# Cross attention of a two-layer decoder trunk: plain fp32 matmuls replaced by three fp32r passes over high and low parts

## The reference

```python
def memory_attention(h, m, wq, wkv, wo):
    q = (h @ wq).reshape(B, S, X_HEADS, X_HEAD_DIM).astype(F32)
    kv = (m @ wkv).reshape(B, M, 2, X_HEADS, X_HEAD_DIM).astype(F32)
    s = jnp.einsum('bshe,bmhe->bhsm', q, kv[:, :, 0]) * (X_HEAD_DIM ** -0.5)
    p = jax.nn.softmax(s, axis=-1)
    o = jnp.einsum('bhsm,bmhe->bshe', p, kv[:, :, 1]).reshape(B, S, D_MODEL)
    return o.astype(h.dtype) @ wo
```

## Time and profile before

| | us |
|---|---|
| median of 3 runs (lowest to highest) | 1506.36 (1506.22 to 1506.47) |
| the profiled execution's own time | 1506.58 |
| its span in the profile | 1504.5 |
| TensorE (PE) busy | 1483.1 |
| VectorE (DVE) busy | 882.4 |
| ScalarE (ACT) busy | 634.4 |
| GpSimd (POOL) busy | 380.3 |

### The profile page before, as it was taken

How to read it: one execution, slowest core, us unless ns; L and a number is a source line. 1 busy time by engine, 2 the same in 40 slices (tenths; PEclk the granted TensorE clock), 3 DMA queues, 4 the chain that set the end, 5 groups by cost and what they waited for, 6 DMA issues and landing times.

```text
span 1504.5 us, 19092 instructions
## 1 busy us (share of the span) xinstructions
PE 1483.1 (99%) x7842; PEld 1267.1 (84%) x7842; DVE 882.4 (59%) x1010; ACT 634.4 (42%) x883; POOL 380.3 (25%) x272
## 2 busy tenths in 40 slices
PE   8999999999999999999999999999999999999997
PEld 7878898888898888888898888988888988888886
DVE  5345556724367666575982465756245585756658
ACT  6335424524344343443562454335344352434344
POOL 2001720300053422315030028102001715151422
PEclk9999999999999999999999999999999999999999
DMA  8333131431223424152343232135203342433402
GB/s 288 90 98 101 53 112 65 150 122 54 94 106 115 137 85 162 62 168 99 112 133 119 64 95 86 67 105 175 84 29 112 112 147 79 141 110 112 140 28 98
DMA packets 83237, 162.09 MB, mean 108 GB/s; under 512 B 3664, under 2 KB 19792, under 8 KB 83152
## 3 DMA queue, kind: packets, MB, share of 16 engines
q1 hardware_dynamic: 81712, 158.35, 31.5%
q10 hardware_dynamic: 1440, 2.53, 0.5%
HBM read 158.78 MB, written 2.10 MB: 107 GB/s over the span
## 4 chain that ended last, share of the span: by engine, by line
PE 94%; DVE 2%; DMA 1%; ACT 1%; issue 1%; POOL 0%; SPq 0%; POOLq 0%; DVEq 0%; ACTq 0%
PE proj L688 26%; PE proj L690 25%; PE proj L689 25%; PE work L888 2%; PE work L690 2%; PE work L688 2%; PE work L689 2%; PE work L717 2%; PE work L867 2%; PE work L753 1%; DMA w_raw<-in_x_wkv_dram 1%; PE work L764 1%; PE work L743 1%; PE work L842 1%; PE work L821 0%
## 5 line engine op out<-in xcount | busy, mean ns | idle before, releaser
L1379 DVE TENSOR_TENSOR w_lo<-w_raw,w_hi 128x2048 fp32r<-128x2048 f32 (+1 forms) x103 | 234.8, 2280 | 274.9 <-ACT w_hi L1078 274.6
L688 PE MATMUL proj<-hT_hi,w_hi 128*128 128x512 f32 (+1 forms) x800 | 298.5, 373 | 0.0
L689 PE MATMUL proj<-hT_lo,w_hi 128*128 128x512 f32 (+1 forms) x800 | 297.7, 372 | 0.0
L690 PE MATMUL proj<-hT_hi,w_lo 128*128 128x512 f32 (+1 forms) x800 | 297.7, 372 | 0.0
L1078 ACT ACTIVATE w_hi<-w_raw 128x2048 fp32r<-128x2048 f32 (+1 forms) x103 | 185.3, 1799 | 234.2 <-PE proj L690 232.2
L688 PE MATMUL proj<-w_hi,hT_hi 128*128 128x512 f32 (+1 forms) x640 | 238.5, 373 | 3.5 <-ACT kmT L1182 2.2
L690 PE MATMUL proj<-w_hi,hT_lo 128*128 128x512 f32 (+1 forms) x640 | 232.3, 363 | 0.0
L689 PE MATMUL proj<-w_lo,hT_hi 128*128 128x512 f32 (+1 forms) x640 | 231.8, 362 | 0.0
L690 PEld LDWEIGHTS proj<-hT_hi,w_lo 128*128 128x128 f32 x800 | 150.7, 188 | 26.3
L689 PEld LDWEIGHTS proj<-hT_lo,w_hi 128*128 128x128 f32 x800 | 150.7, 188 | 26.1
L688 PEld LDWEIGHTS proj<-hT_hi,w_hi 128*128 128x128 f32 x800 | 150.7, 188 | 26.0
(11 more groups left out here) (197 smaller groups left out, 2446.3 us busy)
## 6 DMA issues: line engine op xcount, KB each, us to landing
w_raw<-in_w_up_dram SPq DMA_DIRECT2D x32, 1024.0 KB, 5.7
w_more<-in_w_down_dram SPq DMA_DIRECT2D x24, 1024.0 KB, 5.1
w_raw<-in_w_in_dram SPq DMA_DIRECT2D x28, 768.0 KB, 4.4
w_raw<-in_x_wkv_dram SPq DMA_DIRECT2D x15, 1024.0 KB, 5.1
w_raw<-in_w_out_dram SPq DMA_DIRECT2D x8, 1024.0 KB, 5.0
w_raw<-in_x_wq_dram SPq DMA_DIRECT2D x8, 1024.0 KB, 5.1
w_raw<-in_x_wo_dram SPq DMA_DIRECT2D x8, 1024.0 KB, 5.1
w_hs<-in_w_down_dram SPq DMA_DIRECT2D x8, 1024.0 KB, 5.1
```

The source lines that it names most:

```text
L688: nc.tensor.matmul(dst, l_hi, r_hi, start=first, stop=False, skip_group_check=more)
L689: nc.tensor.matmul(dst, l_hi, r_lo, start=False, stop=False, skip_group_check=more)
L690: return nc.tensor.matmul(dst, l_lo, r_hi, start=False, stop=last, skip_group_check=more)
L1379: nc.vector.tensor_tensor(w_lo[:, slot, :, 0:cols], w_raw[:, raw, :, 0:cols], w_hi[:, slot, :, 0:cols].bitcast(F32), ALU.subtract).then_in ...
```

## The change

The scores and values of the cross attention are made in three fp32r passes. For this the queries, the keys, the values and the transposed probabilities each get a high and a low part. New on ScalarE: one copy of `kmT` (2048 elements in each partition). New on VectorE in each layer: one subtraction for `kmT_lo` (2048), 8 for `qx_lo`, 4 for `vm_lo` and 8 for `xpT_lo` (512 each). A bank of `proj` used by `vm` and `qx` jobs, and bank 2 of `work`, are now free when VectorE has made the low part, and no longer when ScalarE has copied.

The values are made in 8 rounds, round r = (two token tiles r // 2, head r % 2 of the pair): 2 chunks by 2 memory tiles by 3 passes of 256 columns. A round stands three steps behind the scores, not two, so there is a step 10; it stands after the first tile of the second block of `wo0`. On ScalarE the order in a step is now `hT_hi`, copy, exps. Lines left out are declarations of semaphores, start counts and the like; `...` in a `rearrange` stands for its pattern.

```diff
+X_SPLIT_JOBS = ("qx0", "qx1")
+VM_SPLIT_JOBS = ("vm0", "vm1")
 # bank_users(): the last user of a bank of proj
+            elif name in X_SPLIT_JOBS:
+                last[t] = ("qx_lo", 4 * X_SPLIT_JOBS.index(name) + t)
+            elif name in VM_SPLIT_JOBS:
+                last[t] = ("vm_lo", MT * VM_SPLIT_JOBS.index(name) + t)
+ROUND_LAG = 3
+def round_of(r):
+    both, i = divmod(r, 2)
+    pair, t = divmod(2 * both, T)
+    first = pair * BK + 2 * i
+    return both, i, slice(first, first + 2), slice(t * P, (t + 2) * P)
...
-        vm = part("vm", 8, [P, MT, D])
+        vm_hi = part("vm_hi", 8, [P, MT, D], F32R)
+        vm_lo = part("vm_lo", 0, [P, MT, D], F32R)
-        x_probsT = part("x_probsT", 20, [P, 2, 512])
+        xpT_hi = [part(f"xpT_hi{i}", at, [P, 2 * MT, 2 * P], F32R) for i, at in enumerate((20, 40))]
+        xpT_lo = nc.alloc_sbuf_tensor_at("xpT_lo", [P, 2, 2 * MT, 2 * P], F32R, offset=mem_start)
-        qxT = part("qxT", 24, [P, KC, S])
+        kmT_lo = part("kmT_lo", 60, [P, KC, MEM], F32R)
+        kmT_hi = nc.alloc_sbuf_tensor_at("kmT_hi", [P, KC, MEM], F32R, offset=hs_start)
+        qx_hi = part("qx_hi", 24, [P, KC, S], F32R)
+        qx_lo = part("qx_lo", 44, [P, KC, S], F32R)
...
 # TensorE, x_scores (the head of a unit, its two chunks k)
+                    pe.wait_ge(km_lo, nth(km_lo, l, 1))
-                pe.wait_ge(emptied, nth(emptied, l, TILES_BEFORE["qx1" if pair == 0 else "wo0"]))
+                pe.wait_ge(qx_lo_done, nth(qx_lo_done, l, 4 * (pair + 1)))
-                        mm = nc.tensor.matmul(work[:, u % 2, i * MEM:(i + 1) * MEM], qxT[:, c, t * P:(t + 1) * P],
-                                              kmT[:, c, :], start=(k == 0), stop=(k == 1))
+                        mm = three_passes(work[:, u % 2, i * MEM:(i + 1) * MEM], qx_hi[:, c, tokens], qx_lo[:, c, tokens],
+                                          kmT_hi[:, c, :], kmT_lo[:, c, :], k == 0, k == 1)
 # x_turn
-                pe.wait_ge(x_copied, nth(x_copied, l, u))
+                pe.wait_ge(xp_lo_done, nth(xp_lo_done, l, u))
 # x_weigh(l, r)
+                pe.wait_ge(xp_lo_done, nth(xp_lo_done, l, 2 * both + 2))
                 pe.wait_ge(x_lo, nth(x_lo, l, r))
+                pe.wait_ge(vm_lo_done, nth(vm_lo_done, l, 2 * MT))
+                for n, k in enumerate(range(chunks.start, chunks.stop)):
                     for j in range(MT):
+                        mm = three_passes(work[:, 3, n * 2 * P:(n + 1) * 2 * P], vm_hi[:, j, at], vm_lo[:, j, at],
+                                          xpT_hi[both % 2][:, i * MT + j], xpT_lo[:, both % 2, i * MT + j],
+                                          j == 0, j == MT - 1)
 # x_step
-                if 2 <= j < XUNITS + 2:
-                    x_weigh(l, j - 2)
+                if ROUND_LAG <= j < XUNITS + ROUND_LAG:
+                    x_weigh(l, j - ROUND_LAG)
 # before_tile of wo0 and its second block; after_tile
-                    pe.wait_ge(x_lo, nth(x_lo, l, (b - FIRST_BLOCK["wo0"]) * T + t + 1))
+                    pe.wait_ge(x_lo, nth(x_lo, l, (b - FIRST_BLOCK["wo0"]) * T + 2 * (t // 2) + 2))
+                if b == FIRST_BLOCK["wo0"] + 1 and t == 0:
+                    x_step(l, XUNITS + 2)
...
 # ScalarE, x_step: the old order was exps, hT_hi, copy
+                if j >= ROUND_LAG:
+                    act.wait_ge(x_weighed, nth(x_weighed, l, j - ROUND_LAG + 1))
+                    nc.scalar.activation(hT_hi[:, chunks, tokens], work[:, 3].rearrange(...), ACT.Copy).then_inc(x_hi, 1)
+                if 1 <= j <= XUNITS:
+                    act.wait_ge(x_turned, nth(x_turned, l, u + 1))
+                    act.wait_ge(x_weighed, nth(x_weighed, l, 2 * both - 2))
+                    nc.scalar.activation(xpT_hi[both % 2][:, :, u % 2 * P:(u % 2 + 1) * P],
+                                         work[:, 2].rearrange(...), ACT.Copy).then_inc(x_copied, 1)
                 if j < XUNITS:                                    # the two exps, as before
...
 # ScalarE, before_block
+                if b == FIRST_BLOCK["qx0"] + 1:
+                    act.wait_ge(turned, nth(turned, l, 2 * TURNED["n2", T - 1] + 2))
+                    nc.scalar.activation(kmT_hi[:], kmT[:], ACT.Copy).then_inc(km_hi, 1)
 # VectorE, x_step: first in the step
+                if 2 <= j <= XUNITS + 1:
+                    dve.wait_ge(x_copied, nth(x_copied, l, u + 1))
+                    nc.vector.tensor_tensor(xpT_lo[:, u // 2 % 2][dst], work[:, 2].rearrange(...),
+                                            xpT_hi[u // 2 % 2][dst].bitcast(F32), ALU.subtract).then_inc(xp_lo_done, 1)
 # VectorE, new helpers
+            def vm_low(l, name, t):
+                dve.wait_ge(emptied, nth(emptied, l, TILES_BEFORE[name] + t + 1))
+                nc.vector.tensor_tensor(vm_lo[:, t, at], proj[:, t], vm_hi[:, t, at].bitcast(F32),
+                                        ALU.subtract).then_inc(vm_lo_done, 1)
+            def qx_low(l, name, t):
+                dve.wait_ge(emptied, nth(emptied, l, TILES_BEFORE[name] + t + 1))
+                nc.vector.scalar_tensor_tensor(out=qx_lo[:, c], in0=proj[:, t], scalar=XD ** -0.5,
+                                               in1=qx_hi[:, c].bitcast(F32), op0=ALU.mult,
+                                               op1=ALU.subtract).then_inc(qx_lo_done, 1)
 # VectorE, after_tile: first of all
+                for name in X_SPLIT_JOBS:
+                    if b == FIRST_BLOCK[name] + KB - 1:
+                        qx_low(l, name, t)
+                for name in VM_SPLIT_JOBS:
+                    if b == FIRST_BLOCK[name] + KB - 1:
+                        vm_low(l, name, t)
 # VectorE, before_block
+                if b == FIRST_BLOCK["qx0"] + 1:
+                    dve.wait_ge(km_hi, nth(km_hi, l, 1))
+                    nc.vector.tensor_tensor(kmT_lo[:], kmT[:], kmT_hi[:].bitcast(F32), ALU.subtract).then_inc(km_lo, 1)
```

More of the change, by code:

```diff
@@ L486, in trunk @@
         qk_lo = counted("qk_lo", 2 * PAIRS)
+        qx_lo_done = counted("qx_lo_done", 2 * 4)
+        km_hi = counted("km_hi", 1)
+        km_lo = counted("km_lo", 1)
         den_turned = counted("den_turned", UNITS)
@@ L509, in trunk @@
         x_turned = counted("x_turned", XUNITS, 2)
-        x_copied = counted("x_copied", XUNITS, 1)
+        x_copied = counted("x_copied", XUNITS)
+        xp_lo_done = counted("xp_lo_done", XUNITS, 1)
+        vm_lo_done = counted("vm_lo_done", 2 * MT)
         x_weighed = counted("x_weighed", XUNITS, 2)
@@ L861, in x_scores @@
                     pe.wait_ge(turned_lo, nth(turned_lo, l, 2 * TURNED["n2", T - 1] + 2))
-                pe.wait_ge(emptied, nth(emptied, l, TILES_BEFORE["qx1" if pair == 0 else "wo0"]))
+                    pe.wait_ge(km_lo, nth(km_lo, l, 1))
+                pe.wait_ge(qx_lo_done, nth(qx_lo_done, l, 4 * (pair + 1)))
                 pe.wait_ge(x_exped, nth(x_exped, l, u - 1))
+                tokens = slice(t * P, (t + 1) * P)
                 for i in range(2):
@@ L876, in x_turn, with x_weigh @@
                 mm.then_inc(x_turned, 1)
[L878 to L886, removed]
+            def x_weigh(l, r):
+                both, i, chunks, _ = round_of(r)
+                pe.wait_ge(xp_lo_done, nth(xp_lo_done, l, 2 * both + 2))
+                pe.wait_ge(x_lo, nth(x_lo, l, r))
+                pe.wait_ge(vm_lo_done, nth(vm_lo_done, l, 2 * MT))
+                for n, k in enumerate(range(chunks.start, chunks.stop)):
                     for j in range(MT):
-                        mm = nc.tensor.matmul(work[:, 3, k * P:(k + 1) * P], vm[:, j, (pair * BK + k) * P:(pair * BK + k + 1) * P],
-                                              x_probsT[:, u % 2, (i * MT + j) * P:(i * MT + j + 1) * P],
-                                              start=(j == 0), stop=(j == MT - 1))
+                        at = slice(k * P, (k + 1) * P)
+                        mm = three_passes(work[:, 3, n * 2 * P:(n + 1) * 2 * P], vm_hi[:, j, at], vm_lo[:, j, at],
+                                          xpT_hi[both % 2][:, i * MT + j], xpT_lo[:, both % 2, i * MT + j],
+                                          j == 0, j == MT - 1)
                 mm.then_inc(x_weighed, 1)
@@ L1045, in _ @@
                                     pe.wait_ge(qk_lo, nth(qk_lo, l, user[1] + 1))
+                                elif user[0] == "vm_lo":
+                                    pe.wait_ge(vm_lo_done, nth(vm_lo_done, l, user[1] + 1))
+                                elif user[0] == "qx_lo":
+                                    pe.wait_ge(qx_lo_done, nth(qx_lo_done, l, user[1] + 1))
                                 else:
@@ L1061, in _ @@
         def _(act):
-            start_counts(act, emptied, p_copied, c_copied, x_exped, x_copied)
+            start_counts(act, emptied, p_copied, c_copied, x_exped)
             act.dma_start(gains[:, GAIN_SLOT["mem"]], norm_g[0:1, GAIN["mem"]].broadcast_to([P, D])).then_inc(gain_loaded["mem"], 16)
```

(30 more changed lines are left out.)

7 lines of the change are left out of this document (4 added, 3 removed).

## The result

The changed kernel takes 1508.89 us (median of 20 runs, 1508.34 to 1508.96), the kernel before beside it 1506.30 (1506.11 to 1506.49). The ratio is 1.0016, with an interval of 1.0010 to 1.0023: 2.6 us slower, where 2.8 were forecast. So the change did save matmul time, and new waits of TensorE gave back more than it saved.

The account below looks back on a forecast made before the run. TensorE, busy for 99% of the span, bounds the kernel. Per layer −5.04 us of matmuls, +4.1 of step waits and +2.4 of vm waits give +1.4; two layers +2.8 on 1506.36: 1509.2 us, range 1504.0 to 1512.0.

Parts of the forecast that it names:

- A pass of 256 columns takes 0.120: Cross-attention scores and values: 0.120 us per fp32r pass, saving 5.04 us per layer, 10.1 in two.
- rival 3: Cross-attention matmuls: passes start 0.109 us apart by the page's rule, giving 1506.6 us, no change; chance 0.05.
- The vm jobs wait 2.4 us a layer: Start of vm1 and qx0: TensorE waits for vm_low behind VectorE's list, 1.87 and 0.32 us plus restarts.
- Transposes 0, 1 and 5 wait 0.9, 1.2 and 1.7: Steps 1, 2 and 6 of cross attention: TensorE waits 0.90, 1.20 and 1.71 us for the normalised probabilities.
- Values 0 and 2 wait 0.09 and 0.27: Steps 3 to 5: values wait for xpT_lo of units 1 and 3, 0.09 and 0.27 us.
- The new subtraction takes 0.69: VectorE low parts written in strips of 128: seen after 0.69 us, as hT_lo; high bound 1.28.
- rival 4: New VectorE subtraction is slow, 1.28 us, lengthening waits: 1513.6 to 1514.8 us, half of it 1511.5; chance 0.15.
- kmT and the queries cost nothing: qx0's second block: kmT copy and kmT_lo fit idle time; query low parts come early, except the last tile's.
- no wait in steps 7 to 10: Late cross-attention steps: a 2.73 us tile between them covers more than the step's chain lacks, cost nothing.
- Total waits some 13 us above before: All TensorE waits over the whole kernel: predicted some 13 us above those of the kernel before.
- +1.4 us for each layer: Net per layer: −5.04 matmul saving, +4.1 waits in the steps, +2.4 waits at the vm jobs.
- Rival 1: Both layers: the new waits hide and the 10.1 us saving arrives whole, 1496.3 us; chance 0.12.

Follow-up runs that it names:

- the kernel without low parts: Changed kernel with VectorE making no low parts of keys, queries, values or probabilities; same matmuls read the high part twice, not exact: 1499.73 us.
- the banks: Changed kernel with the two tiles of vm1 moved to banks 2 and 3 of proj: 1504.01 us.
- The second and third experiments: Changed kernel with, on VectorE, qx_low of the last query tile behind step 1: 1506.95 us; with xpT_lo 4 and normalisation 5 ahead of w_lo: 1505.38 us.
- the mended order: Changed kernel with vm1 in banks 2 and 3, steps 0 to 3 in qx1's second block, step 6's front ahead of w_lo, query low parts earlier: 1495.52 us.
- The 64-column kernel: One-tile-per-step version of the changed kernel with each values pass halved again, 48 passes of 64 columns in a step: 1615.88 us.
- the one-tile kernel: Changed kernel with values made for one token tile and both heads in a step, 24 passes of 128 columns: 1525.05 us.

## Why the prediction was right

It said +2.8 us and the runs gave +2.6. Its steps, one by one:

- *A pass of 256 columns takes 0.120.* Right: 343.28 to 343.40. The saving is 10.4 us by a steady step, 10.5 by busy time and 10.6 by the kernel without low parts, against 10.1 forecast. Starts 0.109 apart (rival 3) are refuted by the trace after as by the one of before.
- *The vm jobs wait 2.4 us a layer.* Right, and shown by the banks: −5.0 for both layers. The first matmul of vm1 came at 291.88. All of this trace runs 0.44 us earlier at this point than before (normalisation 289.86 against 290.30), so it came 2.01 late against 1.97 forecast.
- *Transposes 0, 1 and 5 wait 0.9, 1.2 and 1.7.* The list has 0.78, 1.10 and 1.57, which with the hidden 0.16 are 0.94, 1.26 and 1.73. Transposes 5 started at 374.12 + 0.44 = 374.56; the walk with the vm waits gives 372.03 + 2.39 = 374.42. The second and third experiments took the first and the last of them away, at 2.0 and 3.6 us against 1.8 and 3.4 to 3.6.
- *Values 0 and 2 wait 0.09 and 0.27.* The trace has 0.15 and 0.30.
- *The new subtraction takes 0.69.* Right (rival 4 wrong):

```profile
L1681 DVE TENSOR_TENSOR xpT_lo<-work,xpT_hi 128x512 fp32r<-128x512 f32 x16 | 11.0, 685 | 2.3 <-ACT xpT_hi L1249 2.3
```

- *kmT and the queries cost nothing; no wait in steps 7 to 10.* Right: the list has no other new wait.
- *Total waits some 13 us above before.* Right, but the list alone doesn't say so. It has 10.9 against 0.7, and eight waits more bring 8 × 0.26 that it hides, and the four short gaps 0.9: 13.2.
- *+1.4 us for each layer.* Right, to 0.1. The 0.44 must be known for this. The trace of the kernel before has it from the first 30 us on: ScalarE makes the second block's w_hi when the weights have come by DMA, and that was 0.41 later there. The first of these rows is of before, the second of after:

```profile
23.98 1.91 ACT L1078 ACTIVATE w_hi<-w_raw 128x2048 fp32r<-128x2048 f32 x1 [1.86 <-DMA w_raw<-in_x_wkv_dram]
23.57 1.91 ACT L1111 ACTIVATE w_hi<-w_raw 128x2048 fp32r<-128x2048 f32 x1 [1.63 <-DMA w_raw<-in_x_wkv_dram]
```

In the traces of the experiments it starts at 23.54 to 23.83. Of the kernel before there is one trace only, so whether the change or that execution did this is open. The cross attention itself is read between the 0.44 and a row of the next layer, then between that row and the last matmul, each pair with before first:

```profile
937.39 0.38 PE L821 MATMUL work<-qkT 64*128 64x128 f32 x2
938.36 0.38 PE L846 MATMUL work<-qkT 64*128 64x128 f32 x2
...
1494.82 0.39 PE L690 MATMUL proj<-w_hi,a_lo 128*128 128x512 f32 x1
1497.18 0.39 PE L715 MATMUL proj<-w_hi,a_lo 128*128 128x512 f32 x1
```

Layer 1 costs 0.97 + 0.44 = 1.41, layer 2 2.36 − 0.97 = 1.39, together the 2.8 forecast. The traces' spans differ by only 2.3 since 0.44 goes off at the start. That the medians differ by 2.6, so near to 2.8, is chance in its last tenths.

- *Rival 1* (the saving arrives whole) is what the mended order does. It wasn't wrong about what is possible, but about this kernel's lists.

The chances put "the same" just ahead of slower, since 2.8 us is just under the 0.2%. The interval (0.10% to 0.23%) stays clear of zero, so twenty runs do tell this difference from none.

## What to carry to other kernels

Here work was moved from a full engine to one that is 59% busy, and it paid only where it came early enough in that engine's list. Before such a change, look at each new instruction for what stands ahead of it in its own list and who waits behind it; here the same 40 small subtractions cost 2.6 us in one order and let 11.0 us through in another. Where a bank is now released by a second engine, try another bank first: here it took four waits and 5.0 us away.

## What the runs showed of the hardware

The fp32r passes of this kernel have a floor. The next start came after 0.227 us at 512 columns, 0.120 at 256, and 0.111 at 128 and at 64. So taking two token tiles at once was the part of the change that made it worth trying: at 128 columns the values alone need 24 × 0.111 = 2.7 us a step, more than the fp32 1.78. The Trainium skill (TensorE: Matmul & The Clock Gate, section "Wait — 56ns, not 53.3ns?") has 55.6 ns for 128 columns and a floor of 25 ns for small ones. These fp32r passes, each with weights of its own, show neither: 111 ns at both sizes. What sets the floor wasn't tested. Each pass has its own weight load, and the records of these start 0.11 us apart too.

The 64-column kernel lost its clock. The granted share (1.00 is 2.4 GHz, 0.50 is 1.2 GHz, values between are a mix of the two) in its stretches (us from the span's start, us, TensorE busy (records), clock, share of DMA, GB/s):

```profile
357.00:362.90 5.90, 5.90 (x55) 1.00 0.00 0
362.90:370.00 7.10, 7.10 (x50) 0.74 0.01 2
370.00:380.00 10.00, 10.00 (x63) 0.67 0.00 0
380.00:390.00 10.00, 10.00 (x38) 0.50 0.01 2
```

```profile
362.92 0.40 PE L711 MATMUL work<-xpT_hi,vm_hi 128*128 128x64 f32 x1
363.14 0.40 PE L712 MATMUL work<-xpT_lo,vm_hi 128*128 128x64 f32 x1
```

The 64-column passes began at 357.96, behind the scores. TensorE had no idle time from 356.04 on, and at 362.9, within these passes, the clock fell to 1.2 GHz; a start then took 0.21 us in place of 0.111 (362.92 to 363.14 above). It rose again at 366.3, in the middle of the next scores, and fell once more at 369.7, within the next 64-column passes. At the lower level 256 columns take the same 0.21:

```profile
365.76 0.41 PE L711 MATMUL work<-kmT_hi,qx_hi 128*128 128x256 f32 x1
365.97 0.41 PE L712 MATMUL work<-kmT_lo,qx_hi 128*128 128x256 f32 x1
```

The cross attention of the one-tile kernel, with 128 columns, keeps a clock of 1.00 (340 to 400 and 1100 to 1200). A lower stretch comes only behind it, 0.83 from 1210 to 1220, after a wait of 2.1 us for VectorE; that profiled execution took 1528.99 us, 4 more than the other three. What it is in the 64-column passes that brought the clock down was not looked into.
